# Modulation products beside the feed-forward matmuls: row chunks multiplied and added on VectorE, ScalarE and GpSimd instead of TensorE

## The reference

```python
mx = (s_lat @ ada_w[l] + ada_b[l]).reshape(bsz, N_MOD, 1, d)   # N_MOD = 9, ada_w[l] is 1024 x 9216
mc = (s_ctx @ ada_w[l] + ada_b[l]).reshape(N_MOD, d)
x = x + 0.5 * mx[:, 2] * swiglu(ada_norm(x, norm_g[l, 0], mx[:, 0], mx[:, 1]), ffn_w_in[l, 0], ffn_w_out[l, 0])
```

## Time and profile before

| | us |
|---|---|
| median of 3 runs | 2388.71 (2387.81 to 2392.62) |
| span of the profiled execution | 2386.5 |
| TensorE busy (matmuls) | 2292.2, 96% of the span |
| VectorE busy | 1157.7, 49% |
| ScalarE busy | 856.4, 36% |
| GpSimd busy | 158.3, 7% |
| mean granted TensorE clock | 0.981 |

### The profile page before, as it was taken

The page is one execution under the profiler, slowest core; times in us unless marked ns, Lnnn a source line. Parts: engine busy times, 40 slices in busy tenths (PEclk is TensorE's granted clock), DMA queues, the critical chain, the costliest instruction groups (busy, mean ns, idle before and its releaser), DMA issues. The chain is left out here.

```text
span 2386.5 us, 36154 instructions
## 1 busy us (share of the span) xinstructions
PE 2292.2 (96%) x13814; PEld 1876.8 (79%) x13814; DVE 1157.7 (49%) x1955; ACT 856.4 (36%) x1390; POOL 158.3 (7%) x138
## 2 busy tenths in 40 slices
PE   6999999999999999988899999999999999998998
PEld 4777797887777788856787777788888887978998
DVE  5226365653333454366553433355343346476665
ACT  4125454632222233247431221233222234455544
POOL 0003112100000010040200000010000010001000
PEclk8999999999999999988999999999999999998999
DMA  9653444455665344500355565343333233224573
GB/s 303 188 159 110 152 140 104 124 151 154 186 189 150 114 142 118 151 16 19 106 150 150 179 191 168 101 119 89 88 97 106 81 93 92 79 80 115 170 208 116
DMA packets 514695, 313.04 MB, mean 131 GB/s; under 512 B 15899, under 2 KB 513138, under 8 KB 514454
## 3 DMA queue, kind: packets, MB, share of 16 engines
q1 hardware_dynamic: 513992, 311.33, 44.4%
q10 hardware_dynamic: 590, 0.16, 0.0%
HBM read 310.41 MB, written 1.05 MB: 131 GB/s over the span
## 5 line engine op out<-in xcount | busy, mean ns | idle before, releaser
L1035 PE MATMUL ps<-h_hi,w_hi 128*128 128x512 f32 (+1 forms) x2064 | 747.1, 362 | 12.1 <-DVE w_lo L1841 3.7
L1035 PE MATMUL ps<-h_hi,w_lo 128*128 128x512 f32 (+1 forms) x2064 | 736.7, 357 | 0.0
L1035 PE MATMUL ps<-h_lo,w_hi 128*128 128x512 f32 (+1 forms) x2064 | 736.5, 357 | 0.0
L1841 DVE TENSOR_TENSOR w_lo<-stage,w_hi 128x1024 fp32r<-128x1024 f32 x227 | 283.0, 1249 | 390.2 <-ACT w_hi L1364 389.9
L1035 PEld LDWEIGHTS ps<-h_hi,w_hi 128*128 128x128 f32 x2064 | 391.4, 190 | 99.1 <-issue 34.4
L1035 PEld LDWEIGHTS ps<-h_hi,w_lo 128*128 128x128 f32 x2064 | 391.4, 190 | 62.4
L1035 PEld LDWEIGHTS ps<-h_lo,w_hi 128*128 128x128 f32 x2064 | 391.8, 190 | 58.3
L1364 ACT ACTIVATE w_hi<-stage 128x1024 fp32r<-128x1024 f32 x227 | 236.9, 1055 | 366.6 <-PE ps L1035 252.1
L1841 DVE TENSOR_TENSOR w_lo<-deep,w_hi 128x1024 fp32r<-128x1024 f32 x184 | 225.3, 1234 | 243.4 <-ACT w_hi L1364 242.3
L1364 ACT ACTIVATE w_hi<-deep 128x1024 fp32r<-128x1024 f32 x184 | 190.8, 1054 | 160.3 <-PE ps L1035 117.8
L1035 PE MATMUL ps<-g_hi,w_hi 128*128 128x512 f32 (+1 forms) x638 | 234.1, 367 | 0.4
(11 more groups left out here) (405 smaller groups left out, 2928.1 us busy)
## 6 DMA issues: line engine op xcount, KB each, us to landing
modw<-in_ada_w SPq DMA_DIRECT2D x72, 1024.0 KB, 6.0
stage<-in_ffn_w_in SPq DMA_DIRECT2D x88, 512.0 KB, 5.0
deep<-in_ffn_w_in SPq DMA_DIRECT2D x88, 512.0 KB, 4.1
modw<-in_w_mod SPq DMA_DIRECT2D x18, 1024.0 KB, 7.7
stage<-in_w_in SPq DMA_DIRECT2D x30, 512.0 KB, 5.0
stage<-in_ffn_w_out SPq DMA_DIRECT2D x32, 384.0 KB, 3.5
stage<-in_even_w_in SPq DMA_DIRECT2D x24, 512.0 KB, 4.0
deep<-in_ffn_w_out SPq DMA_DIRECT2D x32, 384.0 KB, 3.5
```

What stands on the lines that cost most here:

```text
L1035: last = mm(ps[:, j, 0:b - a], w_part[wp][:, u % RING, c, :], x_part[xp][:, x, a:b], start=first and wp == xp, stop=final and wp == "lo")
L1841: up(V.tensor_tensor(w_lo[:, u % RING], arrival(u)[0], w_hi[:, u % RING].bitcast(F32), ALU.subtract), "w_ready", rounds)
```

## The change

In the phases with `vec=True` (the 52 segments above) two segments form a *pair* of 512 columns. VectorE multiplies each of the eight row chunks (128 rows by 512 columns, a row in each partition) with the latent scalar of its rows and adds it to the accumulator `acc[0]`. ScalarE multiplies the same chunk in place with the context scalar, and GpSimd adds those into `acc[1]`. TensorE then only sums the accumulators over the partitions, by four matmuls with ones. Bias, transposes and a copy to `modT` follow as before, once a pair. A pair is loaded in two halves of 1 MB. All chunks are handled in two *pieces* of four.

```diff
@@ plan
+            if vec:
+                pairs = hosted["mod_sum"]
+                r.update({"vec_dve": 8 * pairs, "vec_act": 8 * pairs, "vec_pool": 7 * pairs})
...
+        modv = over("modv", "modw", 0, [P, 2, KC // 2, 2 * SEG])
+        pairb = sb("pairb", [P, SEG])
+        acc = [work[:, 1536:2048], work[:, 2048:2560]]
...
+        def paired_at(p, j, js):
...
+            return {2: (None, None, None, 0), 4: (None, 0, None, 1)}[k["hper"]][j]
+        def pieces_at(p, j, js):
...
+            return {2: (((0, 0),), ((0, 1),), (), ()), 4: (((0, 0), (0, 1)), (), ((1, 0), (1, 1)), ())}[k["hper"]][j]
+        def dve_piece(eng, p, i, q, s, rounds):
+            m, per_turn = p.kw["host"], p.kw["hper"]
+            if s == 0:
+                eng.wait_ge(S("unit_done"), p.at("unit_done"))
+                eng.wait_ge(S("mod_rows"), i * per_turn + (p.at("mod_rows") + 2 * q))
+            piece_full(eng, p, i, q, s)
+            for n in range(KC // 2):
+                k = s * (KC // 2) + n
+                scale = svec[:, m["block"], k, 2:3]
+                if k == 0:
+                    up(V.tensor_scalar(acc[0], modv[:, s, n, :], scale, None, ALU.mult), "vec_dve", rounds)
+                else:
+                    eng.wait_ge(S("vec_dve"), i * (4 * per_turn) + (p.at("vec_dve") + 8 * q + k))
+                    up(V.scalar_tensor_tensor(acc[0], modv[:, s, n, :], scale, acc[0], ALU.mult, ALU.add), "vec_dve", rounds)
+        def act_piece(eng, p, i, q, s, rounds):
...
+                eng.wait_ge(S("vec_dve"), i * (4 * per_turn) + (p.at("vec_dve") + 8 * q + k + 1))
+                up(act(modv[:, s, n, :], modv[:, s, n, :], ACT.Copy, scale=svec[:, m["block"], k, 3:4]), "vec_act", rounds)
+        def pool_piece(eng, p, i, q, s, rounds):
...
+            for n in range(0 if s else 1, KC // 2):
+                k = s * (KC // 2) + n
+                eng.wait_ge(S("vec_act"), i * (4 * per_turn) + (p.at("vec_act") + 8 * q + k + 1))
+                if k > 1:
+                    eng.wait_ge(S("vec_pool"), i * (7 * per_turn // 2) + (p.at("vec_pool") + 7 * q + k - 1))
+                up(G.tensor_tensor(acc[1], modv[:, 0, 0, :] if k == 1 else acc[1], modv[:, s, n, :], ALU.add), "vec_pool", rounds)
@@ SyncE: a piece behind the unit of step j
+        def sp_piece(eng, p, i, q, s):
...
+            eng.wait_ge(S("vec_pool"), i * (7 * per_turn // 2) + (p.at("vec_pool") + 7 * q + (0 if s else -4)))
+            eng.dma_start(modv[:, s], w[:, s * (KC // 2):(s + 1) * (KC // 2), cols]).then_inc(mod_full[s], 16)
+            if s:
+                eng.wait_ge(S("mod_sum"), i * (per_turn // 2) + (p.at("mod_sum") + q))
...
+                    eng.dma_start(pairb[64 * n:64 * n + 64, :], b[m["l"]:m["l"] + 1, bias].broadcast_to([64, SEG])).then_inc(mod_full[s], 16)
+                            for q, half in {2: ((), (), ((0, 0),), ((0, 1),)), 4: (((0, 0),), ((0, 1),), ((1, 0),), ((1, 1),))}[k["hper"]][j]:
+                                sp_piece(eng, p, i, q, half)
@@ TensorE, in front of the product of step j
+        def pe_pair_sums(eng, p, i, q, rounds):
+            per_turn = p.kw["hper"]
+            eng.wait_ge(S("vec_dve"), i * (4 * per_turn) + (p.at("vec_dve") + 8 * q + 8))
+            eng.wait_ge(S("vec_pool"), i * (7 * per_turn // 2) + (p.at("vec_pool") + 7 * q + 7))
+            eng.wait_ge(S("mod_sum"), i * (per_turn // 2) + (p.at("mod_sum") + q))
+            for n in range(2):
+                for v in range(2):
+                    j = 2 * n + v
+                    last = mm(ps[32 * j:32 * j + 32, 4, 0:SEG], ones[:, 0:32], acc[v][:, n * SEG:(n + 1) * SEG], start=True, stop=True)
+            up(last, "mod_rows", rounds, by=2)
@@ VectorE, step j of a gemm: pair rows, splits, pieces, evacuation, pair columns
+                    if q is not None:
+                        dve_pair_rows(eng, p, i, q, rounds)
...
+                    for pair, half in pieces_at(p, j, js):
+                        dve_piece(eng, p, i, pair, half, rounds)
                     if not narrow:
                         evacuate(i, j, rounds)
+                    if q is not None:
+                        dve_pair_cols(eng, p, i, q, rounds)
@@ ScalarE, step j: the piece stands between the splits and the evacuation
+                    for pair, half in pieces_at(p, j, js):
+                        act_piece(eng, p, i, pair, half, rounds)
```

More of the change, by code:

```diff
@@ L174, in gemm @@
             r.update(hosted)
-        add("gemm", r, hper=hper, host=host, order=order, w=w, col0=col0, n=n, evac=evac, tok=tok, src=src, ks=ks,
+            if vec:
+                pairs = hosted["mod_sum"]
+                r.update({"vec_dve": 8 * pairs, "vec_act": 8 * pairs, "vec_pool": 7 * pairs})
+        add("gemm", r, hper=hper, vec=vec, host=host, order=order, w=w, col0=col0, n=n, evac=evac, tok=tok, src=src, ks=ks,
             per=per, step=2 if evac == "tok" else 4, row0=row0, fed=fed, peel=peel or not fed or sumsq == "resid", sumsq=sumsq, **kw)
@@ L282, in ffn @@
                     gemm(w_down.pop("w"), 0, KC, "resid", tok=(0, nt), sumsq="resid" if half else None,
-                         fed=not (last and i and half), peel=i and half, hper=hpers[2 * half + 1], **w_down)
+                         fed=not (last and i and half), peel=i and half, hper=hpers[2 * half + 1], vec=True, **w_down)
         w = ("even_w_in_2", 0) if l == 0 else ("odd_w_in_2", 0)
@@ L513, in hosted @@
             k = p.kw
-            every = k["step"] // k["hper"] if k["hper"] else 0
+            every = k["step"] // k["hper"] if k["hper"] and not k["vec"] else 0
             return j // every if every and len(js) == k["step"] and j % every == every - 1 else None
@@ L530, in arrival @@
             return deep[:, v % DEEP], deep_full[v % DEEP], i * (16 * turn // DEEP) + (16 * (v // DEEP) + 16), DEEP
+        def paired_at(p, j, js):
+            k = p.kw
+            if not (k["hper"] and k["vec"] and len(js) == k["step"]):
+                return None
+            return {2: (None, None, None, 0), 4: (None, 0, None, 1)}[k["hper"]][j]
+        def pieces_at(p, j, js):
+            k = p.kw
+            if not (k["hper"] and k["vec"] and len(js) == k["step"]):
+                return ()
+            return {2: (((0, 0),), ((0, 1),), (), ()), 4: (((0, 0), (0, 1)), (), ((1, 0), (1, 1)), ())}[k["hper"]][j]
@@ new lines, in piece_full @@
+        def piece_full(eng, p, i, q, s):
+            each, pair = (16, 48)[s], (p.at("mod_rows") - FIRST) // 2 + q
+            eng.wait_ge(mod_full[s], i * (each * p.kw["hper"] // 2) + each * (pair + 1))
+        def dve_piece(eng, p, i, q, s, rounds):
[12 more added lines that the diff above has]
+                    up(V.scalar_tensor_tensor(acc[0], modv[:, s, n, :], scale, acc[0], ALU.mult, ALU.add), "vec_dve", rounds)
@@ L1507, in dve_cols, with dve_pair_rows, dve_pair_cols @@
             up(last, "mod_kept", rounds)
+        def dve_pair_rows(eng, p, i, q, rounds):
+            eng.wait_ge(S("mod_rows"), i * p.kw["hper"] + (p.at("mod_rows") + 2 * q + 2))
+            up(V.tensor_tensor(modr[:, 0, :], ps[:, 4, 0:SEG], pairb[:, :], ALU.add), "mod_sum", rounds)
+        def dve_pair_cols(eng, p, i, q, rounds):
+            m, per_turn = p.kw["host"], p.kw["hper"]
+            flat = modT[2 * m["block"] + m["l"]][:, :, :].rearrange("p c v -> p (c v)")
+            eng.wait_ge(S("mod_cols"), i * (per_turn // 2) + (p.at("mod_cols") + q + 1))
+            sums = ps[:, 6, 0:2 * P].rearrange("p (c n v r) -> p n c v r", c=2, n=2, v=2)[:, :, :, :, 0]
+            up(V.tensor_copy(flat[:, bass.ds(i * (4 * per_turn) + 4 * (m["seg0"] + 2 * q), 8)].rearrange("p (n c v) -> p n c v", n=2, c=2), sums), "mod_kept", rounds)
         def dve_first(eng, p):
@@ L1990, in pool_gemm @@
                 pool_pairs(eng, p)
+            elif k["hper"] and k["vec"]:
+                for i, js, rounds in turns(eng, k["n"], k["step"], peel=k["peel"]):
+                    for j in js:
+                        for q, half in pieces_at(p, j, js):
+                            pool_piece(eng, p, i, q, half, rounds)
             elif p.kw["sumsq"]:
```

37 lines of the change are left out of this document (29 added, 8 removed).

## The result

The changed kernel takes 2601.2 us (median of 4 runs, 2597.43 to 2602.81), the kernel before 2389.52 in the same runs: 1.0885 times as long, interval 1.0871 to 1.0899. The profiled execution has a span of 2595.6 us and a mean clock of 0.938; before it was 2386.5 and 0.981, so 209.1 us are to be found in the trace. The forecast was 2600.

The account below looks back on a forecast made before the run. TensorE's matmuls bound the kernel, filling 2292.2 of 2386.5 us. Gate-up +98 and down +120 make +218, giving 2604, or 2607 as a median, lowered to 2600 us; range 2480 to 2665.

Parts of the forecast that it names:

- The saving: On TensorE, a pair's sums and transposes cost about 1.05 us instead of 2.6, saving 1.55 us for each of 26 pairs.
- rival D: On TensorE, the fp32 sums cost what the segments did, so 40 us are not saved: 2640 us; chance with forecast 0.73.
- Step 1: Gate-up turn: piece 1 queues behind a split, its adds end at 22.2 us, and TensorE waits 5.5 us from 16.8.
- Step 2: Down projection: both pieces follow the step's second split, adds end at 21.8 us, and TensorE waits 14.1 us from 7.7.
- the alternation: GpSimd adds (1.28 us) and VectorE operations (0.7) take turns; without it the stalls would be 3.9 and 11.1 us.
- Step 3: TensorE's clock falls to half behind stalls, costing 1.5 us a gate-up stall and 2.4 us a down stall.
- A: In gate-up and down, the pieces are done in time and 40 us are saved: 2348 us; chance 0.05.
- B: Only the down projections stall, losing 120 us, while gate-up saves 28: 2480 us; chance 0.12.
- C: ScalarE's and SyncE's queues delay a product a further 3 us in 22 turns, 66 us more: 2666 us; chance 0.10.

Follow-up runs that it names:

- experiment 3: The changed kernel with both pieces of a gate-up turn in step 0, in front of the split of step 1: 2513.09 us.
- experiment 6: The changed kernel with pairs in gate-up only, both pieces in step 0, VectorE's accumulator in PSUM: 2373.19 us; the same with it in SBUF: 2405.11 us.
- experiment 5: The changed kernel with pair sums behind their step's product, bias add behind splits and pieces: 2483.97 us; with down projections hosting on TensorE, 2409.22; then four fillers added, 2398.02.

## Why the prediction was right

**The saving (1.55 a pair).** It was 1.63, measured in turns that don't stall (23.39 against 25.02). TensorE keeps 23.39 - 22.40 = 0.99 us of a pair, where I had 1.05. So rival D is out.

**Step 1 (5.5 us a gate-up turn).** It was 4.9, and its mechanism holds: piece 1 stands behind the split that waits for the interleaved product. With the sums due at 584.49 (589.40 - 4.91), zero is 16.8 earlier, 567.7. Piece 1's first add began at 15.0 (15.2 predicted), and the four adds took 6.6 where I had 1.28 x 4, two multiply-adds and a copy, 6.9. Moving the piece took 88 us away. Not foreseen: the first pairs of two phases wait 7.55 and 8.20. At the first of them piece 0 started 8.5 us behind zero (513.11), where a steady turn starts it at 3.2.

**Step 2 (14.1 us a down pair).** This was the term that was most off: 12.0, and 13.5 at the first pair of each block. The last add ended 19.6 us behind zero instead of 21.8. Most of it lies in the alternation. I had charged a whole VectorE operation (0.7) for each multiply-add that falls between two adds: seven adds in 12.5 us. They took 11.0 (1.28, and six in 9.63). Five multiply-adds did fall between them, as forecast, but each made the chain only 0.3 us longer than the 1.36 from start to start of undisturbed adds. The rest is the start of the first add, 0.6 earlier.

**The port.** Without the alternation the stalls were to be 3.9 and 11.1; with VectorE's accumulator in PSUM they came to 4.07 and 10.57. The first bound was good, the second half a microsecond high. So the way it works was right and its price was not: the alternation stood in my sum with 1.6 and 3.0 us a stall, and taking the accumulator out saved 0.85 and 1.4. The Trainium skill, "SBUF — State Buffer", section "Who interferes with whom", has the lock for a VectorE instruction with two SBUF inputs only against a GpSimd instruction that reads SBUF. By that rule, a PSUM accumulator should free the multiply-adds, and the trace agrees: one in 0.78 us beside GpSimd's adds (six in 4.71), where with two SBUF inputs seven took 10.10 to 10.29.

**Step 3, the clock (1.5 and 2.4).** It was at 0.50 behind every stall of the change, and cost 2.2 us on average behind the short ones as behind the long (1.4 to 2.5 in single stalls). Fillers gave back 52 us; my terms come to 18 x 1.5 + 8 x 2.4 = 46. The gate-up term was 0.7 too small, the down term 0.2 too large.

**The sum.** Waits 192.6, clock 26 x 2.2 = 57, saving 26 x 1.63 = 42: 207, of 209 us between the spans. My terms were 211.8 for the waits, 46 and 40: 218. The stalls were 19 us too long, the clock 11 too short, the saving 2 too small; I had rounded the sum down by 4 to 7, for an alternation that might not be strict. It was strict, and cheaper than I had it. That 2600 came within 2 us of 2601.2 is partly luck: the stalls erred by 19 us one way, the clock by 11 the other way, and the rounding took most of the rest.

**The rivals.** A (2348) was wrong as the kernel is written, but not as a mechanism: it decides from pieces that start 5.5 us sooner, and experiments 3 and 6 moved them. Even then the work wasn't in time until VectorE's port was free too. B (2480) asked for adds of under 0.5 us or an early piece 1; neither was there. C (queues spread the damage, 2666) didn't come out: beyond the sums TensorE's waits come to 92.6 us where the kernel before had 89.6. In the faster versions ScalarE waits for late units, but TensorE doesn't. The TensorE share was forecast at 88% and is 89%, the gate-up turn at 29 to 31 us and is 30.3 on average, 30.5 in steady turns.

## What to carry to other kernels

Moving work from the engine that bounds to engines that are nearly idle is worth its cost there only if the result is ready when the bounding engine comes to it. What matters is where the moved work stands in the queues of its new engines: find the wait in front of it, and start it before that wait, not behind it. A serial chain that runs on VectorE and GpSimd at once should keep VectorE's accumulator in PSUM (experiment 6: 32 us of 2400), and a stall of 4 us or more cost, here, its own length plus 2.2 us of half clock, which matmuls with no purpose but to fill it give back.

## What the runs showed of the hardware that I had not expected

- Behind a stall the clock's price didn't depend on the length: 2.2 us on average after 4.9 and about as much (2.3) after 12 us of idle time. Waits of 1.35 us for the bias add (experiment 5) were followed by half clock at seven of 16 pairs, first pairs left out, and then TensorE went on at 1.0 and was slowed only 1 to 2 us later. In experiment 3 the clock fell at waits of 1.77, 1.86, 2.02, 2.21 and 2.50 us and stayed at 1.0 at 1.85 and 2.77. So at these lengths the length alone didn't decide it.
- GpSimd's adds and VectorE's two-input multiply-adds, in chains with a semaphore between each two, take strict turns, one to one, but a pair of turns is shorter than the two together. In the down projection of the change both start every 1.67 us (an add alone every 1.36, a multiply-add alone every 0.79), where I had 1.28 + 0.7 = 1.98. Taken one by one, a multiply-add (682.67 to 684.31) ends 0.55 us behind the add before it (682.17 to 683.76), and the next add 1.12 us behind that: the first part of each lies under the other.
- ScalarE on 128x512 from SBUF with a scale from a column took 0.72 us in all 208 instructions (L579), not the 0.63 of the square that I had taken it from the earlier trace rows. The Trainium skill, "ScalarE: Activation LUTs", section "What ACT_TABLE_LOAD costs", adds about 93 ns for each scale or bias that is read from a column of a tensor; the two rows differ by 0.09, so they agree, and I had missed it.
